# Attention transposes of two heads' jobs in one PSUM bank and one slot; SSD jobs two at a time in every second slot

## The reference

```python
o = jnp.einsum('bnkgqs,bnskd->bnqkgd', (p / denom).astype(v.dtype), vb)        # attention: probabilities x values
wmat = cb[:, :, None] * segsum_exp(a_cs)                                        # SSD: C·B times exp(differences of sums)
y_diag = jnp.einsum('bgrcls,bcsgrp->bclgrp', wmat, x_)
y = y.reshape(B, S, SSD_D_INNER) * jax.nn.silu(z.astype(jnp.float32))
yg = yg * lax.rsqrt(jnp.mean(yg * yg, axis=-1, keepdims=True) + NORM_EPS)       # gated group norm
```

## Time and profile before

| | |
|---|---|
| median of 3 runs | 1160.22 us (1160.0 to 1160.25) |
| the profiled execution | 1160.4 us, span 1158.6 us |
| PE busy | 1147.2 us, 99% of the span |
| DVE busy | 777.0 us, 67% |
| ACT busy | 601.7 us, 52% |
| POOL busy | 54.0 us, 5% |
| mean granted TensorE clock | 0.999 |

### The profile page before, as it was taken

How to read it: one execution, slowest core, us unless ns; L and a number is a source line. 1 busy time by engine, 2 the same in 40 slices (tenths; PEclk the granted TensorE clock), 3 DMA queues, 4 the chain that set the end, 5 groups by cost and what they waited for, 6 DMA issues and landing times.

```text
span 1158.6 us, 16481 instructions
## 1 busy us (share of the span) xinstructions
PE 1147.2 (99%) x6563; PEld 987.7 (85%) x6563; DVE 777.0 (67%) x1177; ACT 601.7 (52%) x894; POOL 54.0 (5%) x93
## 2 busy tenths in 40 slices
PE   8999999999999999999999999999999999999997
PEld 7988888888998888888889888888889988888886
DVE  7977867977545485665578778669774446666565
ACT  5666655545544454444456666564545444544443
POOL 1000002200000000000000000131000000000000
PEclk9999999999999999999999999999999999999999
DMA  7844455575445365556457443664555444656660
GB/s 231 269 146 139 154 178 196 172 253 180 161 145 170 109 210 190 182 183 206 156 150 235 146 147 126 235 206 163 218 179 166 137 161 125 214 184 196 199 202 36
DMA packets 141703, 204.30 MB, mean 176 GB/s; under 512 B 7348, under 2 KB 79292, under 8 KB 141628
## 3 DMA queue, kind: packets, MB, share of 16 engines
q1 hardware_dynamic: 138596, 198.51, 52.5%
q10 hardware_dynamic: 3032, 4.75, 1.2%
HBM read 202.16 MB, written 1.08 MB: 175 GB/s over the span
## 4 chain that ended last, share of the span: by engine, by line
PE 97%; DVE 1%; ACT 1%; DMA 0%; issue 0%; POOL 0%; POOLq 0%; SPq 0%; ACTq 0%
PE psum L1202 17%; PE psum L1203 17%; PE psum L1205 17%; PE psum L1172 10%; PE psum L1184 6%; PE psum L1185 6%; PE psum L1186 6%; PE psum L1173 5%; PE psum L1227 1%; PE psum L1385 1%; PE psum L1430 1%; PE psum L1453 1%; PE psum L1372 1%; PE psum L1404 1%; PE psum L1412 1%; PE psum L1284 1%
## 5 line engine op out<-in xcount | busy, mean ns | idle before, releaser
L1561 DVE TENSOR_TENSOR w_lo<-raw,w_hi 128x2048 fp32r<-128x2048 f32 (+1 forms) x182 | 407.6, 2244 | 204.7 <-ACT w_hi L770 203.9
L770 ACT ACTIVATE w_hi<-raw 128x2048 fp32r<-128x2048 f32 (+1 forms) x182 | 341.8, 1879 | 192.3 <-PE psum L1205 172.3
L1172 PE MATMUL psum<-act_both,w_hi 128*128 128x512 f32 x512 | 182.1, 400 | 0.0
L1202 PE MATMUL psum<-w_hi,act_both 128*128 128x512 f32 (+1 forms) x384 | 151.9, 395 | 0.2
L1203 PE MATMUL psum<-w_lo,act_both 128*128 128x512 f32 (+1 forms) x384 | 146.4, 381 | 0.0
L1173 PE MATMUL psum<-act_both,w_lo 128*128 128x256 f32 x512 | 143.7, 281 | 0.0
L1205 PE MATMUL psum<-w_hi,act_both 128*128 128x512 f32 (+1 forms) x368 | 140.6, 382 | 0.0
L1184 PE MATMUL psum<-act_both,w_hi 128*128 128x256 f32 x448 | 129.0, 288 | 0.0
L1185 PE MATMUL psum<-act_both,w_hi 128*128 128x256 f32 x448 | 126.7, 283 | 0.0
L1186 PE MATMUL psum<-act_both,w_lo 128*128 128x256 f32 x448 | 126.7, 283 | 0.0
L1172 PEld LDWEIGHTS psum<-act_both,w_hi 128*128 128x128 f32 x512 | 96.2, 188 | 24.6 <-DVE act_both L1590 0.7
(11 more groups left out here) (266 smaller groups left out, 1827.8 us busy)
## 6 DMA issues: line engine op xcount, KB each, us to landing
raw<-in_w_in_dram SPq DMA_DIRECT2D x34, 1024.0 KB, 5.3
raw<-in_w_up_dram SPq DMA_DIRECT2D x32, 1024.0 KB, 5.5
raw<-in_w_down_dram SPq DMA_DIRECT2D x32, 1024.0 KB, 5.1
raw<-in_w_gate_dram SPq DMA_DIRECT2D x24, 1024.0 KB, 5.2
raw<-in_w_ckv_dram SPq DMA_DIRECT2D x16, 1024.0 KB, 5.2
raw<-in_w_br_ssd_dram SPq DMA_DIRECT2D x8, 1024.0 KB, 5.2
raw<-in_w_mix_out_dram SPq DMA_DIRECT2D x8, 1024.0 KB, 5.2
raw<-in_w_cq_dram SPq DMA_DIRECT2D x8, 1024.0 KB, 5.2
```

The costliest lines, as they stand in the source:

```text
L770: act.activation(w_hi[:, slot, 0:n], raw[:, slot, 0:n], ACT.Copy).then_inc(hi_ready.sem, 1)
L1172: pe.matmul(dst, m_hi[:, k, cs], act_both[:, :, k, :], start=k == 0, stop=False)
L1202: pe.matmul(dst, a_hi[:, k0 + k, ts], m_hi[:, k, :], start=first, stop=False)
L1561: dve.tensor_tensor(w_lo[:, slot, 0:n], raw[:, slot, 0:n], w_hi[:, slot, 0:n].bitcast(F32), ALU.subtract).then_inc(lo_ready.sem, 1)
```

## The change

Attention: the transposes of the two jobs of a couple on the first token tile (two transposes each) go into one bank use of YB (columns 0 to 255 and 256 to 511), one after the other in the slot in which the second job's stood, and ACT copies them out with one instruction. The values of couples 0/1 and 8/9 move one slot later, from slots 10 and 18 to 11 and 19 (`valued_at`); those of the other couples stay where they are. SSD: jobs 16 and 17 are masked and exponentiated where they were; of jobs 18 to 23 both of a couple are made in one slot (29, 31, 33), and their products on PE stand in one slot (28, 30, 32, 34). The transposes of closings 4, 5 and 6 stand in slots 30, 32 and 34 behind these products; closing 7's stay in slot 36. POOL's list of jobs between the closings changes to match.

```diff
+def jobs_made(s):
+    if s < job_slot(SSD_JOB0) + 2:
+        return (job_at(s),) if job_at(s) >= 0 else ()
+    n = job_at(s - 2)
+    return (n, n + 1) if n >= SSD_JOB0 + 2 and n % 2 == 0 else ()
+
+def ssd_valued(s):
+    n = job_at(s - 3)
+    return (n, n + 1) if n >= SSD_JOB0 and n % 2 == 0 else ()
+
+def turned_with(n):
+    return n - n % 2 if job_of(n)[1] == 0 else n
+
+def turned_at(s):
+    n = job_at(s - 1)
+    if not 0 <= n < SSD_JOB0:
+        return ()
+    if job_of(n)[1] == 0:
+        return (n - 1, n) if n % 2 else ()
+    return (n,)
+
+def valued_at(s):
+    n = job_at(s - 4)
+    if n in (0, 8):
+        return (n, n + 1)
+    n = job_at(s - 3)
+    return (n, n + 1) if n in COUPLES and n not in (0, 8) else ()
...
-ATTENTION_CLOSINGS, INNER_CLOSINGS, OUTER_CLOSINGS = (0, 1, 2, 3), (6, 7), (4, 5)
-TURN_SLOT = [s + (2 if i in INNER_CLOSINGS else 1) for i, s in enumerate(CLOSE_SLOT)]
+ATTENTION_CLOSINGS, INNER_CLOSINGS, OUTER_CLOSINGS = (0, 1, 2, 3), (7,), (4, 5, 6)
+TURN_SLOT = [s + (1 if i in ATTENTION_CLOSINGS else 2) for i, s in enumerate(CLOSE_SLOT)]
...
-                    for n in ((16, 17, 18), (19, 20), (21, 22), (23,))[c]:
+                    for n in ((16, 17), (18, 19), (20, 21), (22, 23))[c]:
                         weigh(l, n)
...
-                        exps(l, job_at(u))
+                        for n in jobs_made(u):
+                            exps(l, n)
...
-                    if job_at(u - 2) >= SSD_JOB0:
-                        job_values(l, job_at(u - 2))
+                    for n in ssd_valued(u):
+                        job_values(l, n)
...
-                    if 0 <= job_at(u):
-                        job_mask(l, job_at(u))
+                    for n in jobs_made(u):
+                        job_mask(l, n)
```

More of the change, by code:

```diff
@@ L245, in slot_banks @@
         out += [(SB_, ("score", job_at(s), 0)), (TB_, ("score", job_at(s), 1))]
[L246 to L251, removed]
+    for n in turned_at(s):
+        if n == turned_with(n):
+            out.append((YB_, ("probsT", n)))
+    for n in valued_at(s):
+        if n % 4 == 0:
+            out.append((OB_, ("values", n)))
+    if ssd_valued(s):
+        out.append((OB_, ("values", ssd_valued(s)[0])))
     if s == STATES_SLOT:
@@ L882, in turned_probs @@
                     return
-                n_cols = 2 * (job_of(n)[1] + 1) * P
-                act.wait_ge(*is_full(l, ("probsT", n)))
+                couple = job_of(n)[1] == 0
+                if couple and n % 2 == 0:
+                    return
+                key = ("probsT", turned_with(n))
+                act.wait_ge(*is_full(l, key))
                 if n >= 2:
                     act.wait_ge(*values_done.at(l, n - 1))
-                out_of_bank(l, ("probsT", n), pT_sb[:, n % 2, 0:n_cols], bank(("probsT", n))[:, 0:n_cols])
+                if couple:
+                    out_of_bank(l, key, pT_sb[:, :, 0:SEQ], two(bank(key)))
+                else:
+                    out_of_bank(l, key, pT_sb[:, n % 2, :], bank(key))
             def spread(l, n):
@@ L1378, in job_turn @@
                 branch, t, j = job_of(n)
-                key = ("probsT", n)
+                key = ("probsT", turned_with(n))
                 pe.wait_ge(*probs_scaled.at(l, n + 1))
-                pe.wait_ge(*is_free(l, key))
+                if n == turned_with(n):
+                    pe.wait_ge(*is_free(l, key))
                 for i in range(2):
                     for k in range(t + 1):
-                        c, c0 = (i * (t + 1) + k) * P, i * S_HEAD + k * P
+                        c, c0 = (n - turned_with(n)) * SEQ + (i * (t + 1) + k) * P, i * S_HEAD + k * P
                         ins = pe.transpose(bank(key)[:, c:c + P], s_sb[:, n % 2, c0:c0 + P], ident[:])
-                ins.then_inc(full(key), 1)
+                if t == 1 or n % 2:
+                    ins.then_inc(full(key), 1)
             def job_values(l, n):
@@ L1391, in job_values @@
                     opens = n - j
-                    pe.wait_ge(*is_read(l, ("probsT", n)))
+                    pe.wait_ge(*is_read(l, ("probsT", turned_with(n))))
                 else:
@@ L1485, in _ @@
                             job_scores(l, n)
[L1486 to L1490, removed]
+                    for n in valued_at(u):
+                        job_values(l, n)
+                    for n in turned_at(u):
+                        job_turn(l, n)
                     for i, (_, branch, c, g) in enumerate(CLOSINGS):
@@ L1886, in job_mask @@
                 if 2 <= n < 18:
-                    dve.wait_ge(*is_full(l, ("probsT", n - 2)))
+                    dve.wait_ge(*is_full(l, ("probsT", turned_with(n - 2))))
                 elif n >= 18:
```

## The result

| | before | changed |
|---|---|---|
| median of six runs | 1160.24 us (1160.0 to 1161.85) | 1178.01 us (1176.86 to 1179.23) |
| profiled execution, span | 1158.6 us | 1176.0 us |
| mean granted TensorE clock | 0.999 | 0.993 |

The ratio is 1.0154 (95% interval 1.0143 to 1.0164). The direction is as forecast. The size is not: 1171.8 us was forecast, and the range ended at 1177. The profiled execution lost 17.4 us, 8.7 in each of the two layers.

The account below looks back on a forecast made before the run. PE was taken to bound the kernel, holding 97% of the chain. Waits of 6.2 us less gains of 0.4 gave +5.8 us a layer, +11.6 for two: 1171.8 us, own range 1166 to 1175.2, 8-in-10 range 1166.5 to 1177.

Parts of the forecast that it names:

- the third rival: Behind slot 34's wait PE runs at about half rate, costing half of 4.5 us a layer: 1176.3 us; chance 10%.
- job 23's wait: Slot 34: job 23 is ready 1.29 us after job 22, so PE waits 0.45 us more a layer.
- attention joined: Attention slots: joining islands of transposes and values on PE gains 0.3 us a layer, between 0 and 0.6.
- SSD islands joined: SSD slots 27 to 34: fewer separate islands on PE gain 0.1 us a layer, between 0 and 0.4.
- slot 30, jobs 18 and 19: End of slot 30: PE waits for both jobs' multiplications on POOL, 0.65 us a layer, between 0.4 and 0.9.
- slot 32, job 21: End of slot 32: PE waits for job 21 from POOL, 1.1 us a layer, between 0.4 and 1.6.
- slot 34, job 22: Slot 34: masks behind closing 6 and POOL held up by w_lo make PE wait 4.0 us a layer.
- the second rival: Slot 31: DVE's w_lo goes ahead of job 21's multiplication; slot 32 waits 2.2 us more, 1176.2 us; chance 12%.
- "at least nothing": Slot 10's values moved behind slot 11's scores: lower bound, saving nothing if scores-to-values drains the array like leaving a unit.
- The first rival: SSD waits don't bind, only the joined islands' 0.4 us a layer is left: 1159.4 us, not slower; chance 7%.

Follow-up runs that it names:

- fill: Changed kernel plus 32 unread identity transposes on PE in slot 34, ahead of job 22's product: 1172.65 us, ratio 1.0108 to the kernel before.
- masks_early: Changed kernel with masks and exponentials of jobs 18 to 23 one slot earlier, ahead of the closing on DVE: 1160.66 us, ratio 1.0007.
- lo_held: Changed kernel, but in slot 33 DVE holds its w_lo until POOL has done jobs 22 and 23: 1174.52 us, ratio 1.0127.
- evac_first: masks_early with slot 31's gate additions ahead of the closing on DVE in slot 30: 1159.98 us, ratio 0.9997 to the kernel before.
- recips_early: attn_only with job 4's reciprocals ahead of slot 11's w_lo on DVE: 1159.34 us, ratio 0.9992 to the kernel before.
- attn_only: Changed kernel with its SSD half taken back, leaving only the attention half: 1159.84 us, ratio 0.9998 to the kernel before.

## Why the forecast was wrong

**The step that failed is the clock**: the sum has no term for it, and the third rival, "PE's clock falls in the wait of 4 us", stands at 10%. I let the mean clock of 0.999 speak against it, though no wait of this length stands behind the start of the run before, so that nothing had tested it. The clock did fall, in both layers of the profiled execution, and by the mean granted clock (0.991 to 0.993) in every run of the changed kernel. I had half of 4.53 us for it, 2.3 a layer. It was at 0.50 for 6.8 us, of which 6.0 lie behind the wait. There PE's work took 2.9 us longer than at the higher clock, and hid job 23's wait of 0.43: 2.5 net. fill, which keeps the wait and removes the fall, gave back 2.5 in the first layer of its profiled execution and 2.7 by the medians. So the rival's price was nearly right and its chance was not; its 1176.3 lies 1.7 below the measured 1178.01, as the other terms came to 0.4 a layer more than 5.8 and the clock to 0.2 more than 2.3. The range up to 1177 held the rival, but no larger sum beside it.

The Trainium skill's page "TensorE: Matmul & The Clock Gate", section "Why this matters for your kernels", which I set beside that rival, spoke for it: an idle gap between bursts may bring the lower clock. By that rule, the changed kernel's trace agrees: a gap of 4.06 us, then 6.8 us at 0.50.

**The other terms**, a layer, forecast and measured in the first layer of the profiled execution:

| term | forecast | measured |
|---|---|---|
| attention joined | -0.3 | -0.06 |
| SSD islands joined | -0.1 | -0.1 (the rest of the sum) |
| slot 30, jobs 18 and 19 | 0.65 | 0.70 |
| unit 32's bank | none | 0.50 |
| slot 32, job 21 | 1.1 | 0.69 |
| slot 34, job 22 | 4.0 | 4.06 |
| slot 34, job 23 | 0.45 | 0.43 (in fill) |
| lower clock, net of job 23's wait | none | 2.5 |
| sum | 5.8 | 8.7 |

- **Slot 34** was followed correctly through ACT, DVE and POOL: closing 5's transposes start at 221.82, POOL's multiplication 13.69 us later (235.51; forecast 13.63), and job 22's product 16.28 us later (238.10; forecast 16.29). masks_early (no wait once the masks stand ahead) and lo_held (1.3 less without the block) show both parts of it.
- **Slot 32** was sized at 1.1 from an operation of DVE, a `w_lo` or one of the evacuation's, holding POOL up. One of the evacuation's additions did, but only for 0.5 (two multiplications took 2.99 instead of 2.49); with the `w_lo` it was the other way about:

```profile
217.84 2.99 POOL L761 TENSOR_TENSOR s_sb<-s_sb,cbT 128x512 f32<-128x512 f32 x2 [5.25 <-ACT s_sb L950]
```

```profile
218.63 1.07 DVE L1893 TENSOR_TENSOR mg_sb<-mg_sb,tmp 128x512 f32<-128x512 f32 x1
219.62 3.35 DVE L1609 TENSOR_TENSOR w_lo<-raw,w_hi 128x2048 fp32r<-128x2048 f32 x1
```

  POOL was in its second multiplication when DVE came to its `w_lo`, and DVE's operation took 3.35 instead of 2.28. So the second rival ("DVE wins the interface once more") came about only in small: the addition at 218.63 took 1.07 instead of 0.69, as if it stood until the first multiplication was through, and went ahead of the second. The `w_lo` came 1.0 us later and did not. What a `w_lo` does that waits when a multiplication ends, no run tried.
- **Unit 32's bank** I overlooked because I followed only the masks, and not what else now stands behind closing 4's moved low part: closing 5, and behind it the additions that free PE's banks. evac_first, with the additions ahead of both, loses the wait.
- **Attention** gained 0.06 and not 0.3. The joined values and transposes save about 0.3, but job 4's transposes in slot 12 now wait 0.32 us for ACT's `s_sb`, where they waited 0.10 before: 0.2 goes back, and changing from scores to values costs PE 0.31 us (73.82 to 74.13), where the transposes had followed the scores at 0.31 too: nothing is saved there, the "at least nothing" end of my bound. recips_early, without the wait, gains 1.0 us against its own before where attn_only gains 0.2; by PE's starts 0.32 a layer of it is this wait.
- **The first rival** (the waits don't bind) is out by PE's list of waits. As a kernel it is masks_early: 1160.66.

At the higher clock the sum is 6.2 a layer (-0.16 + 0.70 + 0.50 + 0.69 + 4.06 + 0.43), against 5.8 forecast, and fill's profiled execution, 12.2 us longer than that of before (6.1 a layer), agrees. That is near, but partly by luck: 0.50 overlooked and 0.24 of attention not gained stand against 0.41 counted too many in slot 32. With the clock's 2.5 it is 8.7 a layer, 17.4 us.

## What to carry to other kernels

When work is joined into couples on the busiest engine, follow the first product's whole way over the other engines again: here the SSD jobs' masks, behind a closing instead of ahead of it, cost nearly all of the 8.9 us a layer, and moving them ahead again (masks_early) gave back 8.7. Where a forecast holds a wait of several us on PE, add the lower clock behind it as a term and not as a remote case; and where such a wait can't be avoided, matmuls that nobody reads, put into the wait, can be worth their place. Of an operation that is moved, list also the evacuations that now stand behind it.

## What the runs showed of the hardware

- **TensorE's clock in mid-run.** With a wait of 4.06 us, the granted clock was 0.50 (1.2 GHz) for 6.8 us, the last 6.0 of them with PE at work again: 2.5 us lost by fill's first layer. With one of 2.8 us (lo_held) it was 3.4 us in the profiled execution, and more in the others by their mean clocks. With 32 transposes of 128 columns in the wait, 0.11 us apart, and 0.57 and 0.28 us of waits left (fill), it did not fall. The fall doesn't begin with the end of the wait: in the changed kernel it began 0.8 us before it, in lo_held 2.5 and 1.4 us behind it.
- **POOL beside DVE.** A multiplication of 128x512 with two inputs takes 1.25 to 1.30 us on POOL alone; with DVE's `w_lo` running, two took 3.77 instead of 2.49. The other way about, `w_lo` took 3.35 instead of 2.28. In these pairs the one that runs is not slowed, and the one that comes second takes longer by about what the first still has to do. Between two multiplications one of DVE's additions got in (218.63), and the second multiplication took 1.71 us.
